# A mixed chunk in the expert stage, and one choice of experts moved into a projection

## What is computed

```python
q = (xt @ w_q).reshape(T, PEER_HEADS, 2, PEER_DQ // 2)
s1 = jnp.einsum('thc,nc->thn', q[:, :, 0], sub_k1)
s2 = jnp.einsum('thc,nc->thn', q[:, :, 1], sub_k2)
...
top_s, top_j = lax.top_k(cand_s, PEER_TOPK)
idx = jnp.take_along_axis(cand_i, top_j, axis=-1)
g = jax.nn.softmax(top_s, axis=-1)
...
act = jax.nn.gelu(jnp.einsum('cd,ced->ce', xb, u_tab[ib]), approximate=False)
return jnp.einsum('ce,ced->cd', gb * act, v_tab[ib])
```

## Time and profile before

| | |
|---|---|
| median of 3 runs | 3952.82 us (3951.11 to 3956.78) |
| the profiled execution's own time | 3949.0 us |
| its span, first to last instruction | 3947.2 us |
| PE busy | 2912.5 us (74%) |
| DVE busy | 2829.9 us (72%) |
| POOL busy | 1646.3 us (42%) |
| ACT busy | 810.7 us (21%) |
| DMA | 1127.62 MB, mean 286 GB/s |
| gathers by POOL's queue | 673.79 MB of these |

### The profile page before, as it was taken

One profiled execution on the slowest core, in us unless ns is written; L12 is line 12 of the kernel. 1 busy time (PEld: TensorE's weight loads), 2 busy tenths in 40 slices (PEclk: granted clock), 3 DMA queues, 4 the chain that ended last, 5 costly groups with the idle time before them and its releaser, 6 DMA issues.

```text
span 3947.2 us, 40352 instructions
## 1 busy us (share of the span) xinstructions
PE 2912.5 (74%) x14133; PEld 1731.2 (44%) x14161; DVE 2829.9 (72%) x5410; ACT 810.7 (21%) x1885; POOL 1646.3 (42%) x1321
## 2 busy tenths in 40 slices
PE   7479819965999986763996889899798999960000
PEld 5458406553666553421453545465343444420000
DVE  5646485966777566966878969794777666677777
ACT  6334101112222221100110829281000000000000
POOL 5200002233444334744344333342544545667774
PEclk9779959987999898986998999899899999985555
DMA  9369224445878558977698898999999999999996
GB/s 293 117 244 391 91 79 161 154 150 184 268 259 265 186 200 333 369 251 289 218 369 305 266 371 301 382 315 375 359 385 383 390 408 408 407 332 321 315 321 216
DMA packets 309467, 1127.62 MB, mean 286 GB/s; under 512 B 33425, under 2 KB 43281, under 8 KB 305937
## 3 DMA queue, kind: packets, MB, share of 16 engines
q0 software_dynamic: 185040, 673.79, 47.6%
q1 hardware_dynamic: 101184, 358.97, 24.2%
q10 hardware_dynamic: 23040, 92.28, 6.4%
HBM read 996.46 MB, written 128.45 MB: 285 GB/s over the span
## 4 chain that ended last, share of the span: by engine, by line
DMA 22%; DVE 16%; POOL 8%; PE 3%; issue 3%; DVEq 1%; ACT 0%; ACTq 0%
DMA rows<-v,expert_ids 14%; DMA rows<-u,expert_ids 8%; POOL rows L117 8%; DVE rows L143 4%; DVE row_sums L149 4%; DVE branches L1831 3%; PE ps L102 1%; PE ps L104 1%; PE ps L103 1%; PE ps L1679 1%; DVE scores_in L1424 0%; DVE shared_64k L1839 0%; DVE best_key_ids L1355 0%; DVE key_sums L1429 0%; DVE scores_in L1347 0%
## 5 line engine op out<-in xcount | busy, mean ns | idle before, releaser
L117 POOL DMA_INDIRECT rows<-u,expert_ids x640 | 796.2, 1244 | 1335.1 <-DVE hidden_sums L143 821.2
L117 POOL DMA_INDIRECT rows<-v,expert_ids x640 | 770.4, 1204 | 796.9 <-DVE row_sums L149 649.9
L149 DVE SCALAR_TENSOR_TENSOR row_sums<-rows,hidden_sums,row_sums 128x1024 f32<-128x1024 f32 x630 | 796.8, 1282 | 319.3 <-DMA rows<-v,expert_ids 316.3
L1679 PE MATMUL ps<-turned_rows,mixer_state 128*128 128x384 f32 x2048 | 686.1, 495 | 23.0 <-DMA mixer_state<-u_t 22.2
L1716 PE MATMUL ps<-shared_64k 128*128 128x512 f32 x1536 | 669.6, 598 | 43.4 <-DVE shared_64k L1839 43.4
L143 DVE CUSTOM_DVE_ANT_0 rows<-rows,branches 128x1024 f32<-128x1024 f32 x384 | 468.4, 1222 | 174.4 <-DMA rows<-u,expert_ids 169.5
L1679 PEld LDWEIGHTS ps<-turned_rows,mixer_state 128*128 128x128 f32 x2048 | 391.9, 194 | 288.8 <-DMA mixer_state<-u_t 24.1
L1716 PEld LDWEIGHTS ps<-shared_64k 128*128 128x128 f32 x1536 | 294.1, 192 | 418.7 <-issue 418.6
L102 PE MATMUL ps<-x_hi_t_b,shared_64k 128*128 128x384 f16 x912 | 300.6, 330 | 89.5 <-DMA shared_64k<-w_pairs_kept 88.6
L143 DVE CUSTOM_DVE_ANT_0 rows<-rows,x_first 128x1024 f32<-128x1024 f32 x256 | 305.2, 1224 | 43.4 <-DMA rows<-u,expert_ids 40.8
L103 PE MATMUL ps<-x_lo_t_b,shared_64k 128*128 128x384 f16 x912 | 300.3, 329 | 0.0
(11 more groups left out here) (530 smaller groups left out, 4609.6 us busy)
## 6 DMA issues: line engine op xcount, KB each, us to landing
mixer_state<-u_t ACTq DMA_DIRECT2D x128, 512.0 KB, 7.4
shared_64k<-v SPq DMA_DIRECT2D x128, 512.0 KB, 7.7
rows<-strips SPq DMA_DIRECT2D x32, 768.0 KB, 6.7
h_kept<-branches ACTq DMA_DIRECT2D x32, 768.0 KB, 9.9
shared_64k<-weights_kept SPq DMA_DIRECT2D x32, 768.0 KB, 10.9
shared_64k<-h_kept SPq DMA_DIRECT2D x32, 768.0 KB, 14.6
shared_64k<-s_pairs_kept SPq DMA_DIRECT2D x32, 512.0 KB, 6.7
rows<-w_t SPq DMA_DIRECT2D x30, 512.0 KB, 5.6
```

Source lines behind the costliest of these rows:

```text
L117: nc.gpsimd.indirect_dma_start(ring[:, n % NR, :], None, A["u" if r < NSEL else "v"], bass.IndirectOffsetOnAxis(ap=M["idx"][:, c, e:e + 1] ...
L149: nc.vector.scalar_tensor_tensor(acc[:, e % 2, :], src, hid[:, c % 2, e:e + 1], acc[:, e % 2, :], ALU.mult, ALU.add).then_inc(used, 1)
L1679: m = pe.matmul(ps[:, 4 + u % 4, 0:DT], uk[u % 4][:, k, :], x1t[:, k, :], start=k == 0, stop=k == KD - 1)
```

## The change

1. **Chunk 4 becomes mixed** (`HYB = 4`). Its 128 `u` rows go: `NROW` is 1280 - 128 = 1152, and `row_at` says which row is which. Its tokens join the dense tokens in the table stage: each of the 1024 matmuls of `table_block` has 512 columns in place of 384 (`UT`). ACT takes the GELU of the further 128 columns by an instruction of its own and, each two blocks, stores them (128 KB) to a tensor `h_side` in HBM, where the value of each expert and token has a place of 4 bytes. The choice of chunk 4 also works out, for each chosen expert, that place (`M["place"]`). POOL then gathers, for each of the 128 chosen experts, 128 single values of 4 bytes (`gather_values`), one such gather ahead of each row gather from row 878 on (`VALUES_FROM`). Before row 1024, the first `v` row of chunk 4, DVE waits for all of them. The `v` rows stay.
2. **The table of the plan is new**: 2.9 rows a block in the table stage, 2.1 in the value stage. Product 0 stands at row 818, product 31 at row 1080. The spans of the choices are given in blocks; that of chunk 4 is at rows 777 to 870 (before: 737 to 837).
3. **The choice of chunk 1 moves** out of `ffn_head`. The head stores its scores (1 MB) to HBM and waits for that store; the projection of the large group loads them and the key numbers, and DVE makes steps 0 to 95 in the first 6 calls of `rows()` and four steps in each of the next 10. ACT waits for the exponent's input at its block 16, and for the finished choice at block 24, where its buffers are overwritten.

```diff
+HYB = NSP - 1
+UT = DT + P
-NROW = 2 * NSEL * NSP
+NROW = 2 * NSEL * NSP - NSEL
+PROJ_PICKS = [(16 * i, 16 * i + 16) for i in range(6)] + [(96 + 4 * i, 100 + 4 * i) for i in range(10)]
+def row_at(n):
+
+    c = min(n // (2 * NSEL), HYB)
+    return c, n - 2 * NSEL * c + NSEL * (c == HYB)
...
         if r == NSEL:
-            dve.wait_ge(M["hid_gelu"], c + 1)
+            if c == HYB:
+                dve.wait_ge(M["values_in"], 16 * NSEL)
+            else:
+                dve.wait_ge(M["hid_gelu"], c + 1)
...
+        if not g.first:
+            sp.dma_start(M["sco"], A["scores"][1]).then_inc(S["scores_in"], 16)
+            sp.dma_start(M["iota"], A["iota"]).then_inc(iota_in, 16)
...
             if b == 16:
                 act.wait_ge(h_done, 4)
+                if not g.first:
+                    gate_exps(act, M, S, 0)
+            if b == 24 and not g.first:
+                act.wait_ge(M["chosen"], 2)
             evacuate(b)
...
         def rows():
+            for a, b in [next(picks, (0, 0))]:
+                if a < b:
+                    choose(nc, dve, M, S, M["sco"], 1, 0, a, b)
             for a, b in [next(steps, (0, 0))]:
                 use_rows(nc, dve, M, a, b)
...
+        sp.wait_ge(s_out, 8)
+        sp.dma_start(A["scores"][1], sco[1]).then_inc(kept, 16)
+        sp.wait_ge(kept, 16)
...
-        for i in range(NA):
-            choose(nc, dve, M, S, sco[i], i, i, 0, NT)
+        choose(nc, dve, M, S, sco[0], 0, 0, 0, NT)
...
-ROWS_A_BLOCK = 2.3
-CHOICE_SPAN = {5: (2, 48), 6: (60, 112), 7: (124, 178), 3: (188, 252), 4: (288, 388)}
+ROWS_U_BLOCK = 2.9
+ROWS_V_BLOCK = 2.1
+CHOICE_SPAN = {5: (0, 20), 6: (24, 47), 7: (52, 75), 3: (82, 105), 4: (112, 150)}
...
+        def gather_values(e):
+            if e == 0:
+                pool.wait_ge(M["chosen"], HYB + 1)
+                for i in range(2):
+                    pool.wait_ge(side_st[i], 16 * (NBLK // 4))
+            if e < NSEL:
+                nc.gpsimd.indirect_dma_start(
+                    M["hid"][:, HYB % 2, e:e + 1], None, A["h_side"],
+                    bass.IndirectOffsetOnAxis(ap=M["place"][:, e:e + 1], axis=0)).then_inc(M["values_in"], 16)
+
         for n in range(R_MERGE + NR, NROW):
+            if n >= VALUES_FROM:
+                gather_values(n - VALUES_FROM)
             gather_rows(nc, pool, M, A, n, n + 1)
...
-                m = pe.matmul(ps[:, 4 + u % 4, 0:DT], uk[u % 4][:, k, :], x1t[:, k, :], start=k == 0, stop=k == KD - 1)
+                m = pe.matmul(ps[:, 4 + u % 4, 0:UT], uk[u % 4][:, k, :], x1t[:, k, :], start=k == 0, stop=k == KD - 1)
...
-            act.activation(hout[g4 % 2][:, u % 4, :], ps[:, 4 + u % 4, 0:DT], ACT.Gelu).then_inc(h_out, 1)
+            act.activation(hout[g4 % 2][:, u % 4, :], ps[:, 4 + u % 4, 0:DT], ACT.Gelu)
+            if u % 2 == 0 and u >= 4:
+                act.wait_ge(side_st[u // 2 % 2], 16 * (u // 4))
+            act.activation(side[:, u // 2 % 2, u % 2, :], ps[:, 4 + u % 4, DT:UT], ACT.Gelu).then_inc(h_out, 1)
...
+            if u % 2:
+                act.wait_ge(h_out, u + 1)
+                act.dma_start(A["h_side_blocks"][u // 2], side[:, u // 2 % 2]).then_inc(side_st[u // 2 % 2], 16)
```

74 lines of the change are left out of this document (54 added, 20 removed).

## The result

The changed kernel takes **3802.07 us** at the median (3792.78 to 3843.46, 4 runs), the kernel before 3951.97 (3948.25 to 3956.78, 4 runs): a ratio of 0.9649, with a 95% interval of 0.9591 to 0.9708. Two more sets of runs of the same kernel gave 0.9617 and 0.966, so 0.964 is the better figure; two single executions besides took 3811.05 and 3830.79 us.

What follows compares the result with a forecast made beforehand. Three limits in a row: PE with DVE close behind (table stage), PE with DMA full (value stage), rows alone (tail). Terms -23 + 143 + 14 - 296 = -162 gave 3787 us profiled, 3791 us median; range 3755 to 3830 (0.55), wider 3725 to 3875.

Steps and rivals of the forecast that it cites:

- Part 1: Head and projection: moving the choice of chunk 1 gives net -23 us, between -48 and +4.
- The other two steps: Projection: choice steps 96 to 135 between the taps cost +24.7 us; ACT's new waits cost nothing.
- Part 2: Table stage: 512-column matmuls add 220 us on PE, some idle time goes; net +143 us, ends +98 and +220.
- Rival (b): Table stage keeps its idle time (+220), gather pairs cost the full 3.1 us (+60): 3914 us; chance 0.24 with single halves.
- Part 3: Value stage: -26 us from PE's base, +40 from value gathers on POOL's queue; net +14, ends -26 and +60.
- The base of 664: Value stage: 664 us before the cost of value gathers, against 690 before, so -26 us.
- The low end of -26: Value stage: the best case given, -26 us, against the expected +14.
- the +4 of its own cheap pair: Value stage: a row and value gather together at 2.5 us, against 2.45 us a row wanted, add +4 us.
- my two ends: Value stage: a row gather plus a value gather takes POOL between 2.5 us (+4) and 3.1 us (+85).
- Part 4: Tail: 58 rows left at 1.67 us are 97 us, against 393 before: -296 us.
- Rival (a): Gather pair cheap and DVE keeps up: table stage +115, value stage -26, total 3723 us; chance 0.13.
- Rival (c): Value stage: value gather dear, pair 4.8 us, total 4049 us; slower than before from a 4.07 us pair; chance 0.05.

Runs made afterwards that it cites:

- the choice alone: Kernel before, with only the choice of chunk 1 moved, 1280 rows and the old plan kept: ratio 0.9967 to the kernel before.
- Experiment 7: Changed kernel with 132 choice steps ahead of the sigmoid wait and POOL's first five row gathers moved out of the head: 3765.37 us, ratio 0.9546 to the kernel before.
- the second execution: Changed kernel without edit, profiled a second time: span 3793.5 us, against 3841.7 in its first profiled execution.
- experiment 4: Changed kernel without the 128 value gathers and DVE's wait for them: 3738.75 us, ratio 0.9436 to the kernel before.
- experiment 5: Changed kernel with each of the 128 value gathers issued twice: 3959.84 us, ratio 1.0028 to the kernel before.

## Why the prediction held, and where it was off

- **The form of the sum was right**: table stage longer, value stage a little, tail gone. It comes to -153.7 by the spans where I had -162.
- **Part 1, -23, measured -10.7 by the starts of instructions and -13 (-6 to -20) by the runs of the choice alone.** The step that failed: "In the head it takes from 525.32 to 573.16, 47.8 us, which go." The head is shorter by 35.5 only. The removed choice had itself been a cover: POOL's first five gathers, and the 6 us that the block's end takes behind them, ran beside it and are now bare, 12.3 us. Experiment 7 shows it: with the gathers elsewhere the pause is 0.93 us, though only 5 of the 12 us reach PE. I named what the steps cost where they went to, and not what they had hidden where they came from. The other two steps, +24.7 between the taps and nothing for ACT's new wait, come to 24.8 us together.
- **Part 2, +143, measured +131.8.** PE 935 of 949, idle 48 of 45. That the sum is off by 11 us only has some luck in it: the 45 us of idle time that I kept were a guess between the two ends, and 14 us of PE's busy time too many stood against 3 us of idle time too few. Rival (b)'s first half, that all 122 us of idle time stay, is refuted by that.
- **Part 3, +14, measured +28.4 in the second execution.** The base of 664 was right (667.3 in experiment 4); the value gathers cost 51 us and not 40, 33 of them as idle time of PE and 18 as slower instructions at a lower granted clock, for which I had no term. The low end of -26 that I gave leaves out the +4 of its own cheap pair; it should read -22. POOL's pair, 2.87 to 2.90 us, is what the middle of my two ends gives (2.8). In the changed kernel (second execution) a value gather takes 0.95 us at the median and up to 1.99, 1.13 in the mean. The page "SBUF — State Buffer" of the Trainium skill, section "SBUF: two separate sides", has VectorE's instructions with two SBUF inputs and GpSimd's that read SBUF shut each other out of a shared port for a whole instruction. The spread would fit such a lock now and then, the median speaks against one at each gather, and no run here took VectorE's work away to tell.
- **Part 4, -296, measured -302.0.** 53 rows are left and not 58, at the rate that I had.
- **Rival (a)**, a cheap pair, would have been 3723; without any value gather it is 3739. **Rival (c)** was refuted for one gather a row, and its turning point, 4.07 us a row, fits experiment 5, where 4.21 us give a kernel 11 us slower than before.
- What no part had: the stretches of late instructions, up to 42 us of the value stage in one execution and nothing in another. They are the largest part of the difference between 3793 and 3843, with 12 us given back by the tail and 18 us added ahead of the table stage.
- For a profiled execution I had 3787 us; the second took 3795.3 and the first 3843.5. That the second is only 8 us off is partly luck: a start that gained 11 us less and a value stage 14 us longer stand against a table stage 11 us and a tail 6 us better than I had.

## What to carry to other kernels

When work is removed from a place where nothing stood beside it, look again: the small things that it hid (first issues of another engine, a change of blocks, the first loads) remain, and its own length is an upper bound of the gain. Small serial steps that must move should stand ahead of a wait that the engine has anyway; here moving 36 steps, and the exponent that belongs to them, gave 20 us. And an instruction on a queue with slack costs only what goes beyond the slack: the first value gather of a row took the row from below 2.45 us to 2.89 and cost 0.40 us, the second cost its whole 1.30. State the point at which the slack ends, and the pace of whatever stands at counted places behind that queue. Last, a wait that a profile names for nothing should be looked up instruction by instruction: here some were waits for a product and some were not.

## What was not expected of the hardware

- A gather of 128 single values of 4 bytes holds GpSimd as long as one of 128 rows of 4 KB: 0.95 us at the median and 0.30 us of issue, against 0.94 and 0.30. So its price here is one for the instruction, not for bytes, and not for packets either: by the pages' totals for POOL's queue (170704 packets with the value gathers, 166608 without, 185040 before) a value gather leaves 32 packets and a row gather 144. The transfers add nothing that shows, since the DMA engines' share in its stretch is 0.93 and it is 0.99 ahead of it. By the Trainium skill, page "DMA: Bandwidth & Descriptors", section "SWDGE vs HWDGE vs iDMA", GpSimd's cores compute the descriptors of such a transfer in software. Both gathers bring one piece to each of 128 partitions, which would agree with the equal times; no run here counts descriptors or changes the number of pieces.
- TensorE can run short of instructions with nothing to wait for: one matmul instruction in 1.4, 2.1 or 2.8 us, over 54 to 81 us, in three of 14 profiled executions, and for a few us in a fourth. The granted clock then falls (0.61 and 0.53 in the stretches above, 0.99 around them). The cause is open.
